# Gating the prompt rows of an expert's output on VectorE as they leave the accumulators, instead of in the combine, with six norm buffers instead of three

## The chip, the cores and the metric

The kernel runs on one core of one Trainium2 chip. The metric is the device time of one execution in microseconds; smaller is better.

## The reference, cut to what matters

One layer of a decoder trunk for two groups of requests: 1024 prompt rows and 64 sample rows (8 requests of 8 tokens), each of width 1024. Its second half is a mixture of 16 experts with two experts a row, followed by a post-norm:

```
h2 = x * (1 + sc2) + sh2
ff = moe(h2)                 # two experts a row, weights w
x  = layer_norm(ALPHA * x + (1 + g2) * ff, ln_g[1], ln_b[1])
expert: (silu(x @ w_gate[e]) * (x @ w_up[e])) @ w_down[e]
```

The gate `1 + g2` is a vector of 1024 numbers. All prompt rows share one; the sample rows have one for each of the eight requests. It is linear, so that it can be applied to each expert's output row or to the weighted sum of the two.

## The kernel before, in words

The program is a row of blocks, each with one hand-written instruction order for each engine. The last two are touched.

**block_experts (from line 2472).** The rows that chose an expert are packed into *slots* of 128 rows; there are 23 slots here. Every slot has one expert, an expert has one slot or more. All products are made in pieces of float32 split into a high and a low part (the high part is a cast, the low part the difference), three passes for each step of 128. TensorE's loop over the slots (2599 to 2608) is: the gate product of slot s (bank 0), the transposes of the hidden rows a of slot s-1, the up product of slot s (bank 1), the transposes of x for slot s+1, and the down product of slot s-1 (banks 2 and 3). So the down product of a slot runs in the next round of the loop.

ScalarE's `slot` (2645) does silu of the gate product, the high part of aT, the high part of x, and `y_part` (2635), which copies banks 2 and 3 into the staging rows `y` and issues their store to `y_d` in HBM. VectorE's `slot` (2702) does the low part of aT, the product `a` = up x silu, and the low part of x.

In the last slot of each expert both engines also split the next expert's weights (`among(0)`, `among(1)`, `among(2)` for gate, up and down): ScalarE casts two halves of 128x2048 (2622), and VectorE, once each cast half is there, subtracts (2681). The first expert's weights are split ahead of the loop in `first`. SP loads expert e+1's raw weights (2461) when VectorE is through with a part of expert e. After the last expert SP loads the second norm's scale and offset and the gate vector (2537), and the residual rows (2540), into the space of the raw weights. TensorE waits for the low part of x before a gate product, and for the low part of aT and for both copies of `y` (`y_act`, `y_second`) before a down product.

**block_combine (from line 2718).** There are nine tiles of 128 rows, eight of the prompt and one of the sample rows (64). POOL gathers the two expert outputs of each row by 18 indirect DMAs (2766) and then issues the eight outputs (2773): DMAs that add to an output which already holds the norm's offset. Tiles 0 and 1 are weighted and summed by VectorE (2817, 2818), tiles 2 to 8 by TensorE with diagonal matrices that ScalarE prepares (2757, 2781). Then, tile by tile, VectorE multiplies by the gate (2824), adds ALPHA times the residual and takes the row sum (2828); ScalarE makes mean and variance (2793 to 2799); VectorE, one tile behind, subtracts the mean and multiplies by the norm's scale into one of three norm buffers (2838) and takes a reciprocal (2844); ScalarE scales (2787) and POOL writes out. From tile 3 on, line 2838 waits until the output three tiles earlier has landed. The sample tile's offset is added by VectorE (2847), and SP writes it (2866). TensorE waits for the gate multiply four tiles back (2754) before it reuses a pair of banks.

Of the kernel before, what the change touches and what calls it, by code (L numbers as in the profile page):

```python
# [28 lines left out]
P = 128  # L29
D = 1024  # L30
# [165 lines left out]
def memory_experts(c):  # L196

    c.w_lo2, c.x_parts, c.a_parts = allocate(
        c, 1, ("w_lo2", 2 * PART, F32R), ("x_parts", 2 * D, F32R), ("a_parts", 2 * DE, F32R))


def memory_combine(c):

    c.combine, = allocate(c, 2, ("combine", 2 * NT * D + 7 * D + 64 + NT * 2 * P, F32))


def setup(nc, ctx, t):
# [69 lines left out]
    c.modw_in = [c.sem(f"modw_in{s}") for s in range(5)]  # L277
# [7 lines left out]
    o = 0  # L285
# [2186 lines left out]
def block_experts(c):  # L2472
# [16 lines left out]
    c.v_in = sem("v9_in")  # L2489
    hi_done = c.hi_done  # L2490
# [36 lines left out]
    with nc.Block() as block:  # L2527
        @block.sync
        def _(sp):
            with sp.Fori(1, NE) as e:  # L2530
                load_expert(c, sp, e)
# [82 lines left out]
        def _(act):  # L2614
# [20 lines left out]
            def y_part(s):  # L2635

                act.wait_ge(down_done, s + 1)
                act.wait_ge(y_out, s * 16 + 16)
                act.copy(y[:, 0:512], c.bank(2)).then_inc(y_act, 1)
                act.copy(y[:, 512:], c.bank(3)).then_inc(y_second, 1)  # L2640
                act.wait_ge(y_act, s + 1)
                act.wait_ge(y_second, s + 1)
                act.dma_start(c.y_d[bass.ds(s * MB, MB), :], y).then_inc(y_out, 16)

            def slot(s, among):
# [3 lines left out]
                aT_part(s)  # L2649
                among(0)  # L2650
# [8 lines left out]
            def first():  # L2659
                x_part(0)  # L2660
                for h in range(2):
# [6 lines left out]
            aT_part(n)  # L2668
            y_part(n)
# [4 lines left out]
        def _(dve):  # L2674
# [20 lines left out]

            def first():
                split(0, 0, 0, None, (1,))
                x_part(0)
                split(1, 0, 0, None)
                split(2, 0, 0, None)  # L2700

            def slot(s, among):
# [6 lines left out]
                among(1)  # L2709
                among(2)  # L2710
# [4 lines left out]
            aT_part(slots(dve))  # L2715


def block_combine(c):
# [4 lines left out]
    def part(n, count=1):  # L2723
# [4 lines left out]
    nrm = [part(2 * RY + 2 + s) for s in range(3)]  # L2728
    g2s = part(2 * RY + 5)
    x1 = c.raw[:, 0:NT * D].rearrange("p (i d) -> p i d", i=NT)  # L2730
    lng2, lnb2, g2 = (c.raw[:, D * (NT + n):D * (NT + n + 1)] for n in range(3))
    o = (2 * RY + 6) * D
    squares = part(2 * RY + 6)
# [4 lines left out]
    n_ready, scaled, sample_out = sem("n9_ready"), sem("n9_scaled"), sem("y9_sample")  # L2738
    y_in = [sem(f"y9_in{s}") for s in range(RY)]
    done = [sem(f"y9_out{s}") for s in range(3)]  # L2740
    b_done, d_done, y_sum, g2_done, sum_ready, less_done, squared, var_ready, eps_set, link = (
        sem(n) for n in ("b9_done", "d9_done", "y9_sum", "g29_done", "m9_ready", "less9_done", "s9_squared", "v9_ready", "e9_set", "l9"))
# [3 lines left out]
    with nc.Block() as block:  # L2746
        @block.tensor
        def _(pe):
            for i in range(ON_DVE, NT):
# [3 lines left out]
                if i >= 4 + ON_DVE:  # L2753
                    pe.wait_ge(g2_done, i - 3)
# [7 lines left out]
        def _(pool):  # L2762
# [8 lines left out]
            for i in range(smp):  # L2771
                pool.wait_ge(scaled, i + 1)
                pool.dma_start(t["o_y_p"][0, i * P:(i + 1) * P, :], nrm[i % 3], accum_op=ALU.add).then_inc(done[i % 3], 16)

        @block.scalar
        def _(act):
            act.wait_ge(shares, 1)
            for i in range(ON_DVE, NT):
# [3 lines left out]
                a.then_inc(d_done, 1)  # L2782
            act.wait_ge(eps_set, 1)

            def scale(i):
                act.wait_ge(n_ready, i + 1)
                act.activation(nrm[i % 3], nrm[i % 3], ACT.Identity, scale=st[:, 24 * (i % 2) + 16:24 * (i % 2) + 17]).then_inc(scaled, 1)
# [16 lines left out]
        def _(dve):  # L2804
# [7 lines left out]
            def residual(i):  # L2812
                T = tile_rows(i)
                ac = acc[i % 2][0:T, :]
                if i < ON_DVE:
                    dve.wait_ge(y_in[i], 32)
                    linked(dve.tensor_scalar(ac, yy[i][0][0:T, :], c.xw[0:T, i, 0:1], None, ALU.mult))
                    linked(dve.scalar_tensor_tensor(out=ac, in0=yy[i][1][0:T, :], scalar=c.xw[0:T, i, 1:2], in1=ac,
# [5 lines left out]
                dve.tensor_tensor(ac, total, (g2 if i < smp else g2s)[0:T, :], ALU.mult).then_inc(g2_done, 1)  # L2824
                dve.wait_ge(g2_done, i + 1)
# [88 lines left out]
```

## Time and profile before

| | us |
|---|---|
| median of 3 runs | 1234.09 (1234.07 to 1236.64) |
| the profiled execution's own time | 1233.19 |
| its span, first to last instruction | 1231.4 |
| TensorE (PE) busy | 1106.6 (90%) |
| VectorE (DVE) busy | 731.9 (59%) |
| ScalarE (ACT) busy | 587.6 (48%) |
| GpSimd (POOL) busy | 127.0 (10%) |
| mean granted TensorE clock | 0.961 of 2.4 GHz |

Busy time is summed over the whole span. The expert loop runs from about 748 to 1170 us, the combine from about 1173 us to the end.

### The profile page before, as it was taken

What the parts mean: (1) busy time and instruction counts of PE and PEld (TensorE: products, weight loads), DVE (VectorE), ACT (ScalarE), POOL (GpSimd) and SP (SyncE); (2) the same over time, 40 slices, a digit from 0 to 9 for tenths busy, and PEclk for the clock granted to TensorE, in tenths of its full rate; (3) what the DMA queues carried; (4) which work ended last, traced back from release to release, by engine and by line L of the source; (5) the groups of instructions that cost most, each with busy time, mean ns of one, the idle gap of its engine ahead of it and who ended that gap; (6) DMA issues with size and microseconds to landing.
All of it is one profiled execution on the core that took longest, in us unless ns stands there. A gap on an engine that the chain in (4) does not pass through costs nothing. (4 is left out here: it accounts for less than half of the span.)

```text
span 1231.4 us, 20687 instructions
## 1 busy us (share of the span) xinstructions
PE 1106.6 (90%) x7413; PEld 898.3 (73%) x7414; DVE 731.9 (59%) x1433; ACT 587.6 (48%) x1022; POOL 127.0 (10%) x203
## 2 busy tenths in 40 slices
PE   5899999998799999999799927999999999999843
PEld 3898779987566777777587716888888888888621
DVE  1641351342656677776677679885575497556166
ACT  0641101214467767666432245865465576645154
POOL 0321420010100000000000011100000010000061
PEclk9999999999899999999999957999999999999977
DMA  9574773072598000000433368996696699683488
GB/s 348 201 205 156 268 258 125 1 106 71 160 338 196 2 2 2 1 2 1 140 137 120 121 247 313 399 397 245 224 392 220 215 401 399 238 341 123 158 311 150
DMA packets 93111, 238.07 MB, mean 193 GB/s; under 512 B 9430, under 2 KB 18837, under 8 KB 93007
## 3 DMA queue, kind: packets, MB, share of 16 engines
q1 hardware_dynamic: 76921, 189.93, 44.6%
q0 software_dynamic: 10288, 31.20, 8.2%
q10 hardware_dynamic: 5830, 15.99, 3.7%
q8 instruction: 45, 0.74, 0.3%
q14 instruction: 27, 0.22, 0.1%
HBM read 199.04 MB, written 44.33 MB: 198 GB/s over the span
## 5 line engine op out<-in xcount | busy, mean ns | idle before, releaser
L2569 PE MATMUL psum<-w_hi,x_parts 128*128 128x512 f32 x736 | 239.5, 397 | 5.6 <-DVE x_parts L2688 5.6
L2681 DVE TENSOR_TENSOR w_lo<-raw,w_hi 128x2048 fp32r<-128x2048 f32 x95 | 213.3, 2287 | 38.9 <-ACT w_hi L2622 38.0
L2622 ACT CAST w_hi<-raw 128x2048 fp32r<-128x2048 f32 x90 | 168.0, 1920 | 9.5 <-ACT work L2640 9.2
L2569 PEld LDWEIGHTS psum<-w_hi,x_parts 128*128 128x128 f32 x736 | 139.7, 190 | 35.3 <-issue 6.2
L2569 PE MATMUL psum<-w_lo,x_parts 128*128 128x512 f32 x368 | 144.6, 393 | 0.0
L2569 PE MATMUL psum<-w_hi,a_parts 128*128 x368 | 120.3, 398 | 4.0 <-DVE a_parts L2694 4.0
L1763 DVE CUSTOM_DVE_ANT_0 low<-psum,high 128x512 f32<-128x512 f32 (+5 forms) x172 | 92.2, 579 | 37.3 <-PE psum L1451 23.5
L1649 ACT ACTIVATE low<-low,high 128x640 f32<-128x640 f32 (+9 forms) x140 | 98.9, 710 | 10.9 <-DVE high L1763 10.8
L1481 PE MATMUL psum<-keep,low 128*128 128x128 f32 (+1 forms) x556 | 92.3, 286 | 12.1 <-ACT high L1710 6.1
L1676 ACT COPY high<-psum 128x512 f32<-128x512 f32 (+3 forms) x128 | 63.7, 502 | 76.5 <-PE psum L1481 76.3
L716 PE MATMUL psum<-h_hi,l_parts 128*128 128x384 f32 (+1 forms) x384 | 94.1, 328 | 0.0
L2042 PE MATMUL psum<-wo_parts,mix_parts 128*128 128x512 f32 x384 | 93.1, 399 | 0.0
L1481 PEld LDWEIGHTS psum<-keep,low 128*128 128x128 f32 (+1 forms) x556 | 59.8, 140 | 42.5 <-issue 27.4
L2042 PEld LDWEIGHTS psum<-wo_parts,mix_parts 128*128 128x128 f32 x384 | 72.1, 191 | 17.0 <-issue 2.1
L2569 PEld LDWEIGHTS psum<-w_hi,a_parts 128*128 128x128 f32 x368 | 70.0, 190 | 18.2 <-issue 4.2
L2569 PEld LDWEIGHTS psum<-w_lo,x_parts 128*128 128x128 f32 x368 | 69.9, 190 | 14.1
L1499 PE MATMUL psum<-high 128*64 128x128 f32 x1056 | 72.3, 280 | 1.2 <-ACT low L1695 0.7
L2569 PE MATMUL psum<-w_lo,a_parts 128*128 x184 | 72.4, 394 | 0.0
L716 PEld LDWEIGHTS psum<-h_hi,l_parts 128*128 128x128 f32 x384 | 67.6, 188 | 0.7 <-issue 0.4
L2627 ACT CAST x_parts<-psum 128x512 fp32r<-128x512 f32 x48 | 25.8, 590 | 86.5 <-PE psum L2561 86.5
L676 PE MATMUL psum<-l_parts,h_hi 128*128 128x384 f32 (+3 forms) x288 | 64.6, 315 | 1.1 <-DVE h_lo L946 1.1
L1499 PEld LDWEIGHTS psum<-high 128*64 128x64 f32 x1056 | 56.6, 137 | 11.4 <-issue 8.8
(384 smaller groups left out, 1753.5 us busy)
## 6 DMA issues: line engine op xcount, KB each, us to landing
raw<-in_moe_w_gate SPq DMA_DIRECT2D x32, 1024.0 KB, 9.2
raw<-in_moe_w_up SPq DMA_DIRECT2D x32, 1024.0 KB, 9.9
raw<-in_moe_w_down SPq DMA_DIRECT2D x32, 1024.0 KB, 9.1
top<-in_w_mod SPq DMA_DIRECT2D x8, 2048.0 KB, 8.4
y_d<-work ACTq DMA_DIRECT2D x24, 512.0 KB, 6.2
low<-in_w_mod SPq DMA_DIRECT2D x4, 2048.0 KB, 18.9
high<-in_x_prompt SPq DMA_DIRECT2D x16, 512.0 KB, 3.7
y_d<-high SPq DMA_DIRECT2D x1, 8192.0 KB, 24.3
```

What stands on the lines that cost most here:

```text
L676: mm = pe.matmul(stage_bank(n)[0:T, 0:WIDTHS[st]], h_parts[left][:, k, at:at + T], right[:, k, :], start=(k == 0 and left == 0 and right i ...
L716: mm = pe.matmul(piece_bank(pc)[:, 0:w], left[:, k, :], h_parts[right][:, k, toks], start=(k == 0 and left is hi and right == 0), stop=(k ...
L1481: mm = pe.transpose(turn_bank(what)[0:w, (k - 4 * m) * P:(k - 4 * m + 1) * P], pb[n % 3][:, g, k * P:k * P + w], c.ident)
L1499: mm = pe.matmul(c.bank(6 + br)[HD * g:HD * g + HD, j * P:(j + 1) * P], c.vs[:, k0 + k, br, g, :], pT[n % 2][:, g, k, :], start=(k == 0), ...
L1649: act.activation(x, x, ACT.Exp, bias=mx[:, at + g:at + g + 1], scale=-1.0, accum_out=sums[g]).then_inc(e_ev, 1)
L1676: act.copy(dst[:, 0:w], src[:, 0:w]).then_inc(r_act, 1)
L1763: dve.tensor_tensor_reduce(pb[n % 3][:, g, at * P:at * P + cols], c.bank(2 * g + q % 2)[:, 0:cols], bias, -1.0, least if m else 3e38, ALU. ...
L2042: mm = pe.matmul(c.bank(2 * (s % 2) + n), mixed[i % 2][l][:, k, :], wo[w][:, k, n * 512:(n + 1) * 512], start=(k == 0 and l + w == 0), sto ...
L2569: mm = pe.matmul(out, left[l][:, k * P:(k + 1) * P], w[:, bass.ds(at - o + k * step, 512)], start=n == 0, stop=n == len(steps) - 1)
L2622: act.copy(c.w_hi[:, at:at + PART // 2], c.raw[:, o:o + PART // 2]).then_inc(hi_done[p], 1)
L2627: ins = act.copy(xT[0][:, 512 * h:512 * h + 512], c.bank(4 + h))
L2681: dve.tensor_tensor(low, c.raw[:, o:o + PART // 2], c.w_hi[:, at:at + PART // 2].bitcast(F32), ALU.subtract).then_inc(c.lo_done[p], 1)
```

## The change

The gate of the prompt rows moves from the combine into the expert stage. A slot holds prompt rows and sample rows, so a table `row_kind` holds, for each slot and row, a 1 or a 0 for "prompt" and the opposite for "sample". ScalarE writes the multiplier rows (gate for a prompt row, 1 for a sample row) into the staging rows `y`, once the previous store of `y` has landed; VectorE multiplies banks 2 and 3 by them in place. ScalarE only waits and issues the store. The gate vector has a buffer of its own and is loaded at the head of SP's queue of the block. In the combine the gate multiply stays for the sample tile alone, the residual reads the accumulators directly, one multiply of tile 1 goes to ScalarE, and there are six norm buffers. Some semaphores are declared in another way, since more of them are needed.

```diff
+    c.gate_row, c.row_kind = allocate(c, 0, ("gate_row", D, F32), ("row_kind", 2 * (MAX_SLOTS + 1), F32))
...
         @block.sync
         def _(sp):
+            sp.dma_start(c.gate_row, row_broadcast(c.mod_d, 5 * D, D)).then_inc(g2_in, 16)
             with sp.Fori(1, NE) as e:
                 load_expert(c, sp, e)
...
-            for n, src in enumerate((row_broadcast(t["ln_g"], D, D), row_broadcast(t["ln_b"], D, D),
-                                     row_broadcast(c.mod_d, 5 * D, D))):
+            for n, src in enumerate((row_broadcast(t["ln_g"], D, D), row_broadcast(t["ln_b"], D, D))):
...
 (ScalarE)
             def y_part(s):
-                act.wait_ge(down_done, s + 1)
-                act.wait_ge(y_out, s * 16 + 16)
-                act.copy(y[:, 0:512], c.bank(2)).then_inc(y_act, 1)
-                act.copy(y[:, 512:], c.bank(3)).then_inc(y_second, 1)
                 act.wait_ge(y_act, s + 1)
                 act.wait_ge(y_second, s + 1)
                 act.dma_start(c.y_d[bass.ds(s * MB, MB), :], y).then_inc(y_out, 16)
+            def gate_rows(s):
+                act.wait_ge(y_out, s * 16 + 16)
+                act.activation(y, c.gate_row, ACT.Identity, scale=is_prompt[:, bass.ds(s, 1)],
+                               bias=is_sample[:, bass.ds(s, 1)]).then_inc(gated, 1)
             def slot(s, among):
...
                 aT_part(s)
+                gate_rows(s)
                 among(0)
...
             def first():
                 x_part(0)
+                act.wait_ge(g2_in, 16)
+                act.wait_ge(kinds_set, 1)
...
             aT_part(n)
+            gate_rows(n)
             y_part(n)
 (VectorE)
+            def y_part(s):
+                dve.wait_ge(down_done, s + 1)
+                dve.wait_ge(gated, s + 1)
+                dve.tensor_tensor(y[:, 0:512], c.bank(2), y[:, 0:512], ALU.mult).then_inc(y_act, 1)
+                dve.tensor_tensor(y[:, 512:], c.bank(3), y[:, 512:], ALU.mult).then_inc(y_second, 1)
             def first():
                 split(0, 0, 0, None, (1,))
                 x_part(0)
+                dve.memset(is_prompt[:, 0:1], 1.0)
+                dve.memset(is_sample[:, 0:1], 0.0)
+                dve.tensor_scalar(is_prompt[:, 1:], c.ids_i[:, 0:MAX_SLOTS], float(SEQ), None, ALU.is_lt)
+                dve.tensor_scalar(is_sample[:, 1:], c.ids_i[:, 0:MAX_SLOTS], float(SEQ), None, ALU.is_ge).then_inc(kinds_set, 1)
...
                 x_part(s + 1)
                 among(1)
+                y_part(s)
                 among(2)
...
             aT_part(slots(dve))
+            y_part(slots(dve))
 (combine)
-    nrm = [part(2 * RY + 2 + s) for s in range(3)]
+    NN = 6
+    nrm = [part(2 * RY + 2 + s) for s in range(NN)]
+    reused = NT - NN
...
                 if i >= 4 + ON_DVE:
-                    pe.wait_ge(g2_done, i - 3)
+                    pe.wait_ge(sum_ready, i - 3)
...
+            act.wait_ge(y_in[1], 32)
+            act.activation(yy[1][0], yy[1][0], ACT.Identity, scale=c.xw[:, 1, 0:1]).then_inc(half_sum, 1)
...
-                    linked(dve.tensor_scalar(ac, yy[i][0][0:T, :], c.xw[0:T, i, 0:1], None, ALU.mult))
+                    if i == 0:
+                        linked(dve.tensor_scalar(first, first, c.xw[0:T, i, 0:1], None, ALU.mult))
+                    else:
+                        dve.wait_ge(half_sum, 1)
...
-                dve.tensor_tensor(ac, total, (g2 if i < smp else g2s)[0:T, :], ALU.mult).then_inc(g2_done, 1)
-                dve.wait_ge(g2_done, i + 1)
+                if i == smp:
+                    linked(dve.tensor_tensor(ac, total, g2s[0:T, :], ALU.mult))
+                    total = ac
                 dve.wait_ge(c.x1_in[i], 32)
...
-                dve.scalar_tensor_tensor(out=ac, in0=x1[0:T, i, :], scalar=ALPHA, in1=ac, op0=ALU.mult, op1=ALU.add,
+                dve.scalar_tensor_tensor(out=ac, in0=x1[0:T, i, :], scalar=ALPHA, in1=total, op0=ALU.mult, op1=ALU.add,
                                          accum_out=q[:, 0:1]).then_inc(sum_ready, 1)
...
-                if i >= 3:
-                    dve.wait_ge(done[i % 3], 16 * (i // 3))
+                if i >= NN:
+                    dve.wait_ge(done[i - NN], 16)
```

## Rows read from the trace of the kernel before

**Rows 1.** The page: the span, and the costliest group of ScalarE in the expert loop.
```profile
span 1231.4 us, 20687 instructions
PE 1106.6 (90%) x7413; PEld 898.3 (73%) x7414; DVE 731.9 (59%) x1433; ACT 587.6 (48%) x1022; POOL 127.0 (10%) x203
...
L2622 ACT CAST w_hi<-raw 128x2048 fp32r<-128x2048 f32 x90 | 168.0, 1920 | 9.5 <-ACT work L2640 9.2
```

**Rows 2.** Window (us, busy of PE, PEld, DVE, ACT, POOL, PEclk, DMA, GB/s), then TensorE's timeline.
```profile
984.00:1002.00 18.00, 18.00 (x87) 14.97 (x86) 16.06 (x11) 14.42 (x13) 1.83 (x2) 1.00 1.03 397
...
997.03 0.39 PE L2569 MATMUL psum<-w_hi,x_parts 128*128 128x512 f32 x1
...
1009.21 0.48 PE L2569 MATMUL psum<-w_hi,a_parts 128*128 x1
...
1014.75 0.39 PE L2569 MATMUL psum<-w_hi,x_parts 128*128 128x512 f32 x1
```

**Rows 3.** ScalarE's timeline (start, duration, what, [idle before <-releaser]): plain, then split slot.
```profile
867.78 1.07 ACT L2627 CAST x_parts<-psum 128x512 fp32r<-128x512 f32 x2 [5.74 <-PE psum L2561]
...
997.32 0.59 ACT L2639 COPY work<-psum 128x512 f32<-128x512 f32 x1 [0.84 <-PE psum L2569]
...
998.62 0.35 ACTq L2643 DMA_DIRECT2D y_d<-work  x1
999.01 3.72 ACT L2622 CAST w_hi<-raw 128x2048 fp32r<-128x2048 f32 x2 [0.62 <-ACT work L2640]
1002.68 0.60 ACT L2648 ACTIVATE work<-psum 128x512 f32<-128x512 f32 x1
...
1003.64 3.74 ACT L2622 CAST w_hi<-raw 128x2048 fp32r<-128x2048 f32 x2
```

**Rows 4.** VectorE's timeline in the same split slot.
```profile
1000.95 4.50 DVE L2681 TENSOR_TENSOR w_lo<-raw,w_hi 128x2048 fp32r<-128x2048 f32 x2 [1.76 <-ACT w_hi L2622]
1005.36 0.68 DVE L2694 TENSOR_TENSOR a_parts<-psum,a_parts 128x512 fp32r<-128x512 f32 x1
1005.97 4.48 DVE L2681 TENSOR_TENSOR w_lo<-raw,w_hi 128x2048 fp32r<-128x2048 f32 x2
...
1010.97 1.28 DVE L2688 TENSOR_TENSOR x_parts<-psum,x_parts 128x512 fp32r<-128x512 f32 x2
1012.41 4.49 DVE L2681 TENSOR_TENSOR w_lo<-raw,w_hi 128x2048 fp32r<-128x2048 f32 x2 [0.16 <-ACT w_hi L2622]
```

**Rows 5.** Timeline of the combine: TensorE's products, VectorE's wait, and its last tiles.
```profile
1186.03 26.02 PE L2757 MATMUL psum<-combine 128*128 128x512 f32 x56 [17.68 <-DMA combine<-y_d,dest_y]
...
1206.23 1.29 DVE L2838 SCALAR_TENSOR_TENSOR combine<-combine,raw 128x1024 f32<-128x1024 f32 x1 [4.81 <-DMA out_o_y_p<-combine]
...
1216.44 1.23 DVE L2828 SCALAR_TENSOR_TENSOR combine<-raw,combine 128x1024 f32<-128x1024 f32 x1
...
1218.99 1.20 DVE L2824 TENSOR_TENSOR combine<-psum,combine 64x1024 f32<-64x1024 f32 x1
```

**Rows 6.** Windows of the combine's output traffic (last two columns: DMA share, GB/s).
```profile
1199.00:1200.00 1.00, 1.00 (x4) 0.44 (x3) 1.00 (x2) 0.97 (x4) 0.08 (x1) 1.00 1.07 176
...
1204.00:1205.00 1.00, 1.00 (x4) 0.50 (x3) 0.00 (x0) 0.00 (x0) 0.00 (x0) 1.00 1.02 201
...
1215.00:1220.00 5.00, 0.00 (x0) 0.00 (x0) 4.90 (x8) 3.99 (x10) 0.86 (x1) 0.50 0.92 134
```

**Rows 7.** Timeline of the combine: ScalarE's scaling of a normalised tile.
```profile
1191.75 1.13 ACT L2787 ACTIVATE combine<-combine 128x1024 f32<-128x1024 f32 x1
```

**Rows 8.** Timeline at the start of the expert loop, then a window.
```profile
758.61 4.49 DVE L2681 TENSOR_TENSOR w_lo<-raw,w_hi 128x2048 fp32r<-128x2048 f32 x2 [1.04 <-ACT w_hi L2622]
...
765.04 0.49 PE L2569 MATMUL psum<-w_hi,x_parts 128*128 128x512 f32 x1 [3.07 <-DVE x_parts L2688]
...
765.00:770.00 5.00, 4.96 (x15) 3.94 (x16) 4.41 (x2) 4.33 (x4) 0.00 (x0) 0.66 1.04 387
```

**Rows 9.** All 24 stores of the staging rows, from issue to landing.
```profile
DMA to landing us min/median/max: 2.6/6.2/8.3
```

More of the change, by code:

```diff
@@ L275, in setup @@
     c.modT = c.misc[:, 0:144].rearrange("p (a b) -> p a b", a=2 * KT)
-    c.modw_in = [c.sem(f"modw_in{s}") for s in range(5)]
+    c.modw_in = [early_sem(f"modw_in{s}") for s in range(5)]
     c.modb_in, c.mod_half_done = c.sem("modb_in"), c.sem("mod_half_done")
@@ L2489, in block_experts @@
     c.v_in = sem("v9_in")
+    g2_in, kinds_set, gated = sem("g2_in"), sem("kinds_set"), sem("y_gated")
+    is_prompt, is_sample = (c.row_kind[:, (MAX_SLOTS + 1) * n:(MAX_SLOTS + 1) * (n + 1)] for n in range(2))
     hi_done = c.hi_done
@@ L2727, in block_combine @@
     acc = [part(2 * RY + s) for s in range(2)]
-    nrm = [part(2 * RY + 2 + s) for s in range(3)]
-    g2s = part(2 * RY + 5)
+    NN = 6
+    nrm = [part(2 * RY + 2 + s) for s in range(NN)]
+    g2s = part(2 * RY + 2 + NN)
     x1 = c.raw[:, 0:NT * D].rearrange("p (i d) -> p i d", i=NT)
-    lng2, lnb2, g2 = (c.raw[:, D * (NT + n):D * (NT + n + 1)] for n in range(3))
-    o = (2 * RY + 6) * D
-    squares = part(2 * RY + 6)
+    lng2, lnb2 = (c.raw[:, D * (NT + n):D * (NT + n + 1)] for n in range(2))
+    o = (2 * RY + 3 + NN) * D
+    squares = part(2 * RY + 3 + NN)
     o += D
@@ L2737, in block_combine @@
     diag = c.combine[:, o + 64:o + 64 + NT * 2 * P].rearrange("p (i k q) -> p i k q", i=NT, k=2)
-    n_ready, scaled, sample_out = sem("n9_ready"), sem("n9_scaled"), sem("y9_sample")
+    n_ready, scaled, sample_out, once_out = sem("n9_ready"), sem("n9_scaled"), sem("y9_sample"), sem("y9_once")
     y_in = [sem(f"y9_in{s}") for s in range(RY)]
-    done = [sem(f"y9_out{s}") for s in range(3)]
-    b_done, d_done, y_sum, g2_done, sum_ready, less_done, squared, var_ready, eps_set, link = (
-        sem(n) for n in ("b9_done", "d9_done", "y9_sum", "g29_done", "m9_ready", "less9_done", "s9_squared", "v9_ready", "e9_set", "l9"))
+    reused = NT - NN
+    done = [sem(f"y9_out{s}") for s in range(reused)]
+    b_done, d_done, y_sum, sum_ready, less_done, squared, var_ready, eps_set, link, half_sum = (
+        sem(n) for n in ("b9_done", "d9_done", "y9_sum", "m9_ready", "less9_done", "s9_squared", "v9_ready", "e9_set", "l9", "h9_sum"))
     smp = NP_TILES
@@ L2772, in _ @@
                 pool.wait_ge(scaled, i + 1)
-                pool.dma_start(t["o_y_p"][0, i * P:(i + 1) * P, :], nrm[i % 3], accum_op=ALU.add).then_inc(done[i % 3], 16)
+                pool.dma_start(t["o_y_p"][0, i * P:(i + 1) * P, :], nrm[i % NN],
+                               accum_op=ALU.add).then_inc(done[i] if i < reused else once_out, 16)
         @block.scalar
@@ L2786, in scale @@
                 act.wait_ge(n_ready, i + 1)
-                act.activation(nrm[i % 3], nrm[i % 3], ACT.Identity, scale=st[:, 24 * (i % 2) + 16:24 * (i % 2) + 17]).then_inc(scaled, 1)
+                act.activation(nrm[i % NN], nrm[i % NN], ACT.Identity, scale=st[:, 24 * (i % 2) + 16:24 * (i % 2) + 17]).then_inc(scaled, 1)
             for i in range(NT):
@@ L2865, in _ @@
             sp.wait_ge(b_done, 1)
-            sp.dma_start(t["o_y_s"].rearrange("b j d -> (b j) d"), nrm[smp % 3][0:NS, :]).then_inc(sample_out, 16)
+            sp.dma_start(t["o_y_s"].rearrange("b j d -> (b j) d"), nrm[smp % NN][0:NS, :]).then_inc(sample_out, 16)
             sp.wait_ge(c.out_done, c.out_total)
-            for s in range(3):
-                sp.wait_ge(done[s], 16 * ((smp - s + 2) // 3))
+            for s in range(reused):
+                sp.wait_ge(done[s], 16)
+            sp.wait_ge(once_out, 16 * (smp - reused))
             sp.wait_ge(sample_out, 16)
```

10 lines of the change are left out of this document (6 added, 4 removed).

## The prediction

> **What bounds the kernel now.** I read the page first: the span is 1231.4 us and TensorE is busy for nine tenths of it [rows 1]. The profiled execution took 1233.19 us, so 1.8 us lie around the span; the median of the three runs is 1234.09, 0.9 above it. About 0.2% (2.5 us) is what a measurement of this kernel can tell from no change.
>
> The change touches two stages, so I then asked for windows of each. In the expert loop TensorE is busy in all 18 us of the window shown, and a slot lasts 17.7 us, from one gate product (997.03) to the next (1014.75) [rows 2]. But VectorE is busy 16.1 of those 18 us too. It and ScalarE have spare time only in the mean. The reader should look there at the order of work, since both execute strictly in order. In a slot that also splits the next expert's weights (call it a *split slot*), ScalarE does silu, aT high, first weights (two halves), x high, second weights, two copies of the down result, the store's issue, third weights; VectorE does aT low, first, a, x low, second, third [rows 3, 4]. 90 ScalarE splits in the loop are 15 such slots [rows 1]; the other 8 of the 23 are *plain*, seen in the ScalarE timeline by 5.74 us of idle before the x cast in place of 2.1 [rows 3]. In order they are SSSS P S P SS P S P SSSS P SS P S P P: eight times a split slot follows directly on a split slot.
>
> The combine is the other way round: its ends are on VectorE. There TensorE's products run as one group of 26.02 us from 1186.03 and are over at 1212.05, yet VectorE takes the last tile at 1218.99 [rows 5], because each tile costs it a gate multiply, a residual and a normalisation, and it once waits 4.81 us for a norm buffer whose output write had not landed.
>
> **Combine, part by part.** *Removed:* the gate multiply of eight prompt tiles (1.21 us each), one of two operand multiplies of tile 1 (0.75, now ScalarE's, about 1.1, while VectorE works on tile 0), and with six norm buffers the 4.81 us wait, since tile 3 needs no buffer back. VectorE's round falls from 3.8 to 1.22 + 1.28 + 0.16 = 2.7 us [rows 5]. What is late next is TensorE: 26.02 us over seven tiles, less about 2 us at its slow start, are 3.43 us a tile. TensorE itself starts on the landing of tile 2's gathers, which nothing here moves: the gathers keep their place ahead of all outputs on POOL's queue. Its new wait (sum instead of gate multiply four tiles back) asks for tile 4 before tile 8: done near 1200, asked at 1208.6. So the last tile starts at 1212.15 instead of 1218.99. Behind it the order is unchanged (the sample tile keeps its multiply), so the end comes **6.8 us** earlier. Buffers again: tile 6 wants output 0 back at 1210, and it landed by 1206.2; outputs 1 and 2, queued right behind it, need 2.6 us each at the queued rate [rows 6], so they land by about 1211, and are wanted at 1214 and later.
>
> **Expert stage, part by part.** ScalarE loses two copies (1.2 us with their gap, from 997.32 on) and gains a 1024-wide scaled activation, as the combine's norm scaling: 1.13 us [rows 7], right behind aT high. VectorE gains two products from the accumulators, as its x low pair: 1.28 us [rows 4], behind the *second* weights. In sum little: the danger is the order. ScalarE's store, and everything behind it, now waits for VectorE's products, and these wait for VectorE's second weights (1012.41 to 1016.90), where ScalarE's copies (the like of 997.32, a slot later: 1015) ran as soon as the accumulators were ready. The third weights, silu, aT and the next first weights are queued behind that store on ScalarE, and VectorE waits in turn for their halves. That closes a ring. From the end X of x low: second weights X+4.6; gated products X+5.9; store issued and third weights begun on ScalarE X+6.6 (0.62 behind the copy now); two halves 3.67, silu and aT high 0.96, X+11.2; gate rows, X+12.3; first half of the next first weights 1.94, X+14.2; VectorE's two halves and a 5.00, x low 1.28: **X+20.4** [rows 3, 4]. TensorE's own slot is 17.71, so each of the eight direct successions costs 2.7 us: about 1.4 before the gate product (x low late) and 1.3 before the down product, which starts 12.2 us into the slot [rows 2], while aT low is ready at X+13.6.
>
> Before a run, a first split slot behind a plain one has its x low ready 1.5 us early (ring entered at silu, not at the store); after it, the next slot still loses the 1.3. So single split slots cost nothing, and a run of k about 2.7(k-1) - 0.2. Runs of 4, 2, 4, 2: 7.9 + 2.5 + 7.9 + 2.5 = 20.8.
>
> *Start.* TensorE waited 3.07 us for x low at 765.04, the end of a VectorE chain that had waited for ScalarE's first weights [rows 8]; the gate activation stands ahead of these: +1.0. The four small operations before the loop (0.06 to 0.2 us each) fit into the idle time there. The gate vector moves from late on SP's queue to its head, before expert 1's loads, 0.42 us of issue. It delays these by that, unseen since they are used some 12 us after their issue; ScalarE now waits for its landing. The stores of the same 512 KB land in 2.6 to 8.3 us [rows 9]; up to about 4 it is hidden behind x high, at 8.3 it would cost under 3 more. I take none. *Tail.* Two products on VectorE for two copies on ScalarE: 0.3. Lower bound for the stage: 20.8 + 1.0 + 0.3 = **22**, or 21 if the small gaps in the ring close.
>
> *The unknown: the store's landing.* The gate activation overwrites the staging rows, so it waits for the previous store, 5.1 us after its issue in the ring. The 24 stores landed in 2.6 to 8.3 us, median 6.2 [rows 9]; split slots have 6.2 to 8.3. At 2.7 nothing is added, at 6.2 1.1 us in each of eight rings (+9, in all 31), at 8.3 about +25. The loads that share the DMA engines with it (397 GB/s in the window) [rows 2] would be spread over a longer slot and stand some 2 us further ahead of the store, so I take a landing of about 5.5: +3, in all **25**.
>
> The Trainium skill, DMA: Bandwidth & Descriptors, Queues, rings and completion order, says that a DMA engine takes turns packet by packet between the queues that have work. By that rule the store, on ScalarE's queue beside SP's loads, would have half the rate and land in about 4 us (an estimate), the gate rows would never wait, and the sum would be 22. The landings [rows 9] are longer than that wherever loads run, so the rule is not what I count on.
>
> **Sum.** 25 - 6.8 = +18.2 on 1233.19 gives 1251.4; with the 0.9 us of the median, **1252.3**.
>
> **Rivals.**
> *Hidden anyway (faster).* ScalarE waits 2.1 and VectorE 1.8 us in every split slot now [rows 3, 4]; if their added 1.3 us went into those waits, TensorE would never notice, and the combine's gain would stand: 1234.1 + 1.3 - 6.8 = 1228.6. It decides at whether the gated products can run when the accumulators are ready. Against it: at that time VectorE is in the middle of its second weights. Chance 0.08.
> *The clock.* After 3.07 us of waiting the granted clock fell to its lower level (1.2 of 2.4 GHz) for part of the next 5 us, mean 0.66: up to 1.7 us lost [rows 8]. The new waits are 1.2 to 1.5 us, twice a slot. Inside a run the ring hides a slower TensorE; at the end of each of four runs it would cost 1.1 to 1.7: +5, 1257. For it speaks only that longer waits do it; waits this long in a busy stretch aren't in these rows. Chance 0.12. The Trainium skill, TensorE: Matmul & The Clock Gate, HAM oscillation, says that idle gaps between groups of products let the clock fall; by that this case is the one that comes.
> *Slow stores.* At 8.3 us the ring is 23.6 us: about 47 for the stage, 1274. Chance 0.08.
> *Output writes bind the combine.* Alone, each output keeps the DMA engines 0.92 busy over 3.8 us, 3.5 us of engine time; eight of them from about 1199, where the gathers' end lets the rate fall to 176 GB/s, would end near 1227, some 1.6 before those of now: 1257.5. Against it: when queued they moved 201 GB/s, 2.6 us for 0.52 MB, under TensorE's 3.43 [rows 6]. Chance 0.06.
> *No change within 0.2%.* It would need the ring to cost just 6.8, half a run: 0.03.
> The forecast itself, stage +21 to +31: 0.63.
>
> **Range.** The forecast's own is 1248 to 1258, which takes in the clock and the output rival. To hold the time 8 times in 10 it reaches up towards slow stores, 1268, and down to 1243, where the ring would cost half. Slower 0.89, the same 0.03, faster 0.08.
>
> **What would show it.** In the profile after: VectorE's two products right behind its second weights and not behind TensorE; ScalarE's third weights released by VectorE; TensorE waiting on x_parts and a_parts from VectorE some 8 to 12 times each, 1 to 2 us, where it waited twice and once; slots in a run 20.4 us or more apart, plain ones 17.7; a wait of the gate activation on the store or none. In the combine: no wait of the normalisation on an output, VectorE released by TensorE at each tile, 6.8 us from the last product's end less. I am wrong if TensorE does not wait in the runs, or if the last tile in the combine isn't taken right behind its product.

## The result, and the profile after

The changed kernel takes 1268.77 us (median of 4 runs, 1268.07 to 1274.83); the kernel before, run beside it, 1234.08 (4 runs, 1232.16 to 1236.64). The ratio is 1.0284, 95% interval 1.0255 to 1.0313. The forecast was 1252.3, that is +18.2 us, and +34.7 came, 0.8 us beyond the upper end of the range. The sign and the mechanism (a ring through ScalarE's queue) were right, and the size forecast was about half of what came.

The page of the profiled execution (1268.77 us), for [rows 1]. The group of line 2626 is ScalarE's weight splits.

```profile
span 1266.9 us, 20759 instructions
PE 1124.4 (89%) x7413; PEld 908.2 (72%) x7414; DVE 750.9 (59%) x1476; ACT 589.3 (47%) x999; POOL 132.4 (10%) x203
...
L2626 ACT CAST w_hi<-raw 128x2048 fp32r<-128x2048 f32 x90 | 167.2, 1910 | 85.2 <-DVE work L2710 85.2
```

The splits cost the same as before (167.2 us for 168.0), but ScalarE stood idle ahead of them for 85.2 us in place of 9.5, waiting for VectorE's gated product. VectorE's busy time grew by only 19 us, the span by 35.5: what has to be read is the order of work, not the total.

Where the time went: from the first gate product of the loop to the issue of the last store it is 421.45 us before (748.31 to 1169.76) and 463.4 after (746.92 to 1210.34), **+42.0**. From there to the end of the span it is 61.6 before and 56.5 after, **-5.1**. The rest, 1.4, is an earlier start of the loop in this profile; over all the profiles of this case that start lies anywhere from 746.9 to 751.7, so it is not put down to the change.

The chain of waits in the expert stage (engine, what it worked on, who released it: us in total, times, longest):

```profile
ACT w_hi L2626 <- DVE work L2710: 85.2, 15, 6.2
...
DVE w_lo L2691 <- ACT w_hi L2626: 76.1, 29, 3.5
...
ACT work L2648 <- DMA y_d<-work: 37.0, 16, 3.2
...
PE psum L2573 <- DVE x_parts L2698: 29.1, 10, 4.2
...
PE psum L2573 <- DVE a_parts L2704: 6.5, 3, 4.5
```

ScalarE waits for VectorE and VectorE for ScalarE: the ring. The third line is a link that the forecast had weighed and made too small: the gate activation waits for the previous store. TensorE waits ten times for x low instead of twice, and three times for aT low instead of once.

ScalarE in a run of split slots, for [rows 3] (start, duration, what, [idle before <-releaser]):

```profile
793.74 0.35 ACTq L2643 DMA_DIRECT2D y_d<-work  x1
794.13 3.72 ACT L2626 CAST w_hi<-raw 128x2048 fp32r<-128x2048 f32 x2 [6.18 <-DVE work L2710]
797.75 0.60 ACT L2654 ACTIVATE work<-psum 128x512 f32<-128x512 f32 x1
798.24 0.59 ACT L2637 CAST a_parts<-psum 128x512 fp32r<-128x512 f32 x1
801.61 1.24 ACT L2648 ACTIVATE work<-gate_row,row_kind 128x1024 f32<-128x1024 f32 x1 [2.79 <-DMA y_d<-work]
802.76 3.71 ACT L2626 CAST w_hi<-raw 128x2048 fp32r<-128x2048 f32 x2
...
816.80 0.35 ACTq L2643 DMA_DIRECT2D y_d<-work  x1
...
824.34 1.25 ACT L2648 ACTIVATE work<-gate_row,row_kind 128x1024 f32<-128x1024 f32 x1 [2.46 <-DMA y_d<-work]
...
839.53 0.34 ACTq L2643 DMA_DIRECT2D y_d<-work  x1
```

And VectorE in the same stretch, for [rows 4]:

```profile
810.89 4.48 DVE L2691 TENSOR_TENSOR w_lo<-raw,w_hi 128x2048 fp32r<-128x2048 f32 x2
815.30 0.68 DVE L2709 TENSOR_TENSOR work<-psum,work 128x512 f32<-128x512 f32 x1
815.90 0.68 DVE L2710 TENSOR_TENSOR work<-psum,work 128x512 f32<-128x512 f32 x1
819.14 4.49 DVE L2691 TENSOR_TENSOR w_lo<-raw,w_hi 128x2048 fp32r<-128x2048 f32 x2 [2.56 <-ACT w_hi L2626]
```

From store to store it is 23.1 and 22.7 us. The ring is the one forecast at 20.4, and the wait for the store stands in it besides: 2.79 and 2.46 us. In all eight direct successions the distance is the store's landing (6.65 to 7.70 us from its issue, mean 7.25) and 15.36 us more, to within 0.01. The eight last 22.0 to 23.1 us, 22.6 in the mean, instead of 17.7: 39 of the stage's 42 us. The rest is at its ends: the second gate product comes 1.8 us later after the first, and the last store 1.4 us later after the last gate product. A split slot that stands alone costs nothing: around it two slots last 35.43 us from silu to silu (858.83 to 894.26), 17.7 each.

TensorE, the timeline at three gate products of the first run and one of the second, and then windows (us, busy of the engines, granted clock, DMA share, GB/s):

```profile
788.05 0.49 PE L2573 MATMUL psum<-w_hi,x_parts 128*128 128x512 f32 x1 [3.03 <-DVE x_parts L2698]
...
811.12 0.79 PE L2573 MATMUL psum<-w_hi,x_parts 128*128 128x512 f32 x1 [3.47 <-DVE x_parts L2698]
...
833.84 0.79 PE L2573 MATMUL psum<-w_hi,x_parts 128*128 128x512 f32 x1 [2.17 <-DVE x_parts L2698]
...
927.31 0.49 PE L2573 MATMUL psum<-w_hi,x_parts 128*128 128x512 f32 x1 [3.11 <-DVE x_parts L2698]
...
940.83 0.49 PE L2573 MATMUL psum<-w_hi,a_parts 128*128 x1 [0.98 <-DVE a_parts L2704]
```
```profile
788.00:793.00 5.00, 4.95 (x15) 3.94 (x16) 5.00 (x4) 0.00 (x0) 0.00 (x0) 0.66 0.96 309
812.00:818.00 6.00, 6.00 (x18) 4.68 (x18) 4.58 (x4) 0.81 (x1) 0.00 (x0) 0.62 1.06 328
...
927.00:932.00 5.00, 4.69 (x21) 3.89 (x22) 5.00 (x4) 0.22 (x1) 0.00 (x0) 1.00 0.95 306
```

In the first run all of the wait comes at the gate product. With each of these waits the granted clock is at its lower level for some microseconds (1.2 of 2.4 GHz; means of 0.66 and 0.62), so that the up product ends later and the down product finds aT low ready: the second wait that was forecast, 1.3 us before each down product, is used up by slow products. Two gate products show the other case: at 927.31, after 3.11 us of waiting, and at 1065.28, after 1.70, the clock stays at 1.00, and there a wait of 0.98 us does stand before the next down product. So the length of a wait alone does not decide whether the clock falls; what else does was not tried.

The combine, VectorE's timeline and then TensorE's group, for [rows 5]:

```profile
1233.81 1.22 DVE L2860 SCALAR_TENSOR_TENSOR combine<-raw,psum 128x1024 f32<-128x1024 f32 x1 [4.04 <-PE psum L2781]
1234.96 0.08 DVE L2860 DVE_READ_ACCUMULATOR combine<-raw,psum 128x1 f32 x1
1234.96 1.28 DVE L2870 SCALAR_TENSOR_TENSOR combine<-combine,raw 128x1024 f32<-128x1024 f32 x1
...
1240.68 1.22 DVE L2860 SCALAR_TENSOR_TENSOR combine<-raw,psum 128x1024 f32<-128x1024 f32 x1 [0.81 <-PE psum L2781]
```
```profile
1227.23 27.28 PE L2781 MATMUL psum<-combine 128*128 128x512 f32 x56 [18.44 <-DMA combine<-y_d,dest_y]
```

As forecast, VectorE follows TensorE tile by tile, 3.43 us apart, and waits for no norm buffer. From the end of TensorE's group to the end of the span it is 12.4 us in place of 19.3, 7.0 less. But the group is 27.28 us long in place of 26.02, and it ends 44.2 us after the last store's issue (1254.5), where it was 42.3 (1212.05).

### The profile page after: what moved, and what is told of

Same layout as the page of the kernel before. It is cut to its first block and busy times, and to the rows that moved or that the text cites. A ratio compares the mean times of both kernels' runs of the same rounds, so it can differ in the third digit from the quotient of the medians.

```text
span 1266.9 us, 20759 instructions
## 1 busy us (share of the span) xinstructions
PE 1124.4 (89%) x7413; PEld 908.2 (72%) x7414; DVE 750.9 (59%) x1476; ACT 589.3 (47%) x999; POOL 132.4 (10%) x203
## 5 line engine op out<-in xcount | busy, mean ns | idle before, releaser
L2573 PE MATMUL psum<-w_hi,x_parts 128*128 128x512 f32 x736 | 249.7, 412 | 29.1 <-DVE x_parts L2698 29.1
L2626 ACT CAST w_hi<-raw 128x2048 fp32r<-128x2048 f32 x90 | 167.2, 1910 | 85.2 <-DVE work L2710 85.2
L2573 PEld LDWEIGHTS psum<-w_hi,x_parts 128*128 128x128 f32 x736 | 145.5, 198 | 64.4 <-issue 33.1
L2573 PE MATMUL psum<-w_lo,x_parts 128*128 128x512 f32 x368 | 149.2, 406 | 0.0
L2573 PEld LDWEIGHTS psum<-w_hi,a_parts 128*128 128x128 f32 x368 | 70.3, 191 | 21.3 <-issue 7.2
L2573 PEld LDWEIGHTS psum<-w_lo,x_parts 128*128 128x128 f32 x368 | 73.3, 199 | 14.9
L1453 PE MATMUL psum<-score_parts 64*128 64x512 f32 (+3 forms) x528 | 63.7, 365 | 0.0
```

The lines of the kernel that those rows point to most:

```text
L1453: mm = pe.matmul(c.bank(2 * g + q % 2)[:, 0:w * P], left[rows, j, :], right[rows, br, keys], start=n == 0, stop=n == 2)
L2573: mm = pe.matmul(out, left[l][:, k * P:(k + 1) * P], w[:, bass.ds(at - o + k * step, 512)], start=n == 0, stop=n == len(steps) - 1)
L2626: act.copy(c.w_hi[:, at:at + PART // 2], c.raw[:, o:o + PART // 2]).then_inc(hi_done[p], 1)
```

## The experiments

Theory: the ring on ScalarE's in-order queue costs the stage its 42 us, with the gate activation's wait for the store inside it, and the combine's part is a gain. Rivals: the lower clock is the main cost; the combine's part gains nothing; the new work on VectorE and ScalarE costs by itself. The runs were made in three groups, each beside the kernel before, and each ratio is to the kernel before of its own group: 1234.64 us for the first four runs, 1233.14 for the next three and 1234.91 for the last. "Stage" below is from the first gate product to the last store's issue, "end" from there to the end of the span: 421.45 and 61.6 before, 463.4 and 56.5 after.

**Six buffers alone.** The kernel before, with

```diff
-    nrm = [part(2 * RY + 2 + s) for s in range(3)]
+    NN = 6
+    nrm = [part(2 * RY + 2 + s) for s in range(NN)]
```

> The kernel before with six norm buffers in the combine and nothing else; the gate multiplies stay there. Theory (VectorE's order bounds the combine before): the 4.8 us wait of the normalisation of tile 3 goes, VectorE's round stays 3.8 us, so the time falls by 4.8 us to about 1229.3. Rival (output writes bound the end of the combine): the outputs queue up, the wait moves to the end, and the time falls by 1.6 us or less, to 1232.5 or more.

Measured: 1230.57 us, ratio 0.9959 (0.9930 to 0.9987). Stage 422.0, end 58.5. That is 4.1 us less, nearer to the theory's 4.8 than to the rival's 1.6. The wait on an output is gone, and the end is 3.1 us shorter; TensorE's group is 27.44 us here, 1.4 longer than in the profile before, and from its end on 5.1 us are saved, the wait of 4.81 and a little more. This part of the change is a small gain on its own.

**Three buffers in the changed kernel.**

```diff
-    NN = 6
+    NN = 3
```

> The changed kernel with three norm buffers instead of six, the gate still in the expert stage. Theory: the normalisation of tile 3 waits again for output 0, some 5 us, but VectorE's round of 2.7 us under TensorE's 3.43 us a tile catches up 0.7 us a tile over five tiles, so the end is 1 to 3 us later than in the changed kernel: about 1271. Rival (VectorE is the bound as before): the whole wait of 4.8 us is lost, 1273.6 or more.

Measured: 1271.98 us, ratio 1.0324 (1.0273 to 1.0374). The normalisation waits for outputs again, 3.62, 0.96 and 1.20 us, yet the end is 57.4, 0.9 later than with six, and the stage (463.6) the same: the theory's case, at the low end. With the gate multiplies gone VectorE catches up, so the buffers shorten the end by 3.1 us without that part of the change and by 0.9 with it: their gains don't add.

**No wait for the store.** ScalarE does the gate activation into an unused accumulator bank, and VectorE multiplies by the gate vector itself.

```diff
-                act.wait_ge(y_out, s * 16 + 16)
-                act.activation(y, c.gate_row, ...)
+                for h, done in enumerate((half_gated, gated)):
+                    act.activation(c.bank(7), c.gate_row[:, 512 * h:512 * h + 512], ...)
+                    act.wait_ge(done, s + 1)
...
 (VectorE)
+                dve.wait_ge(y_out, s * 16 + 16)
-                dve.tensor_tensor(y[:, 0:512], c.bank(2), y[:, 0:512], ALU.mult)
+                dve.tensor_tensor(y[:, 0:512], c.bank(2), c.gate_row[:, 0:512], ALU.mult)
```

> The changed kernel with the wait on the store out of ScalarE's chain: its gate activations (two of 512 columns, the same work) go to an accumulator bank that nothing reads, and VectorE multiplies by the plain gate vector, so that the sample rows' outputs are gated as prompt rows; the order of the rest is the same. Theory (a ring of 20.4 us in successive split slots, lengthened by the wait for the store to 22.7 to 23.1): slots in a run fall back to about 20.4 us, the stage costs 21 to 24 us more than before instead of 42, total about 1250. Rival (the ring is slow for another reason, such as loads that arrive late or the lower clock): slots in a run stay near 22.7 us and the total near 1268.

Measured: 1257.27 us, ratio 1.0204 (1.0156 to 1.0251). From store to store it is 20.73 to 20.79 us in the eight successions, where 20.4 was worked out; the two half-wide activations take 1.60 us from start to end instead of 1.24, and 1.72 instead of 1.15 up to the start of the next cast, which is more than the rest. The stage is 450.2, end 56.2. TensorE's waits in its profile:

```profile
PE psum L2574 <- DVE x_parts L2700: 17.7, 9, 4.8
PE psum L2574 <- DVE a_parts L2706: 12.0, 9, 4.2
```

In the runs of split slots they are 1.46 to 1.50 us before the gate product and 0.96 to 0.99 before the down product, and the clock stays up: this is the picture that the prediction drew (1.4 and 1.3). So the ring without the store's wait is within 0.4 us of what it was said to be, and taking that wait out is worth 13 us of stage: 1.9 less in each of eight successions, 15 in all, of which some 2 are given back. The stage is still 28.8 us longer than before, not 21 to 24, and the time is 7 us above what was expected of this run. Part of that belongs to the detour: the start waits 4.79 us in place of 4.19, and a split slot behind a plain one, which costs nothing in the changed kernel, takes 0.4 here (silu to silu over two slots 35.80 us for 35.43), six times.

**The gate activation later**, behind x high instead of ahead of the first weights.

```diff
                 aT_part(s)
-                gate_rows(s)
                 among(0)
                 act.wait_ge(up_done, s + 1)
                 x_part(s + 1)
+                gate_rows(s)
```

> The changed kernel with ScalarE's gate activation moved behind its high part of x, out of the way of the first weights; all the rest as it is. Theory: the activation (1.15 us) and the wait for the store leave the ring, which is then 19.3 us, 1.6 over TensorE's slot: the stage costs about 18 us more than before, total about 1245. Rival (only the move of the products to VectorE costs, the place of the activation does not matter): total near 1268. Second rival (the ring is nothing, store traffic is all): total near 1229.

Measured: 1245.90 us, ratio 1.0100 (1.0057 to 1.0143), as expected. From store to store 19.44 to 19.50 us, stage 439.85, end 56.0. The activation now comes 9.5 us behind the store's issue, where it could have started 5.1 behind it, and in the loop it waits for nothing. TensorE's waits are 0.98 us before the down product and 0.20 before the gate product, and the clock is 1.00 behind them:

```profile
798.98 0.50 PE L2573 MATMUL psum<-w_hi,a_parts 128*128 x1 [0.99 <-DVE a_parts L2704]
...
804.91 0.49 PE L2573 MATMUL psum<-w_hi,x_parts 128*128 128x512 f32 x1 [0.20 <-DVE x_parts L2698]
```

What is left of the ring, 1.7 us in each succession, is the store ahead of the third weights.

**The store later too**, behind the third weights. These wait for the down product themselves, so that the store doesn't stand in for that.

```diff
                 among(1)
-                y_part(s)
+                act.wait_ge(down_done, s + 1)
                 among(2)
+                y_part(s)
```

> The changed kernel with both steps taken out of ScalarE's way: the gate activation behind the high part of x, and the store's issue (with its wait for VectorE's products) behind the third weights, which wait for the down product alone. Theory (the ring runs over the third weights queued behind the store, and over the gate activation ahead of the first weights): no ring is left, slots in a run are 17.7 us, the stage costs within 1 us of before, and the combine's gain of 5 to 7 us is seen: about 1228. Rival (VectorE has no room for 1.3 us more in a split slot, whatever the order): slots in a run stay above 18.5 us and the total is 1235 or more.

Measured: **1230.43 us** (12 runs), ratio 0.9975 (0.9958 to 0.9991) of the kernel before: 2.7 us faster, and 38 under the change as it was made. Expected was 1228. Stage 422.97, 1.5 us longer than before, end 55.9. ScalarE in a run:

```profile
795.50 0.60 ACT L2654 ACTIVATE work<-psum 128x512 f32<-128x512 f32 x1 [3.01 <-issue]
...
796.46 3.73 ACT L2626 CAST w_hi<-raw 128x2048 fp32r<-128x2048 f32 x2
800.75 1.08 ACT L2631 CAST x_parts<-psum 128x512 fp32r<-128x512 f32 x2 [0.57 <-PE psum L2565]
801.71 1.26 ACT L2648 ACTIVATE work<-gate_row,row_kind 128x1024 f32<-128x1024 f32 x1
802.86 7.35 ACT L2626 CAST w_hi<-raw 128x2048 fp32r<-128x2048 f32 x4
810.72 0.35 ACTq L2643 DMA_DIRECT2D y_d<-work  x1
```

Second and third weights run back to back (x4), no weight split waits for VectorE, and TensorE's gate products come every 17.7 us, in plain and split slots alike. TensorE waits twice for x low and once for aT low, as before. All of the new arithmetic is in this kernel, so it costs 1.5 us of stage at the most; the other 40 of the change were its place. Six buffers alone (the first run, 1230.57) are as fast: with the gate moved in this way too, the end is 2.5 us shorter but the stage 1 us longer, and the two times can't be told apart.

**The store later, the gate activation as in the change.** The diff of the last run, without that of the one before it.

> The changed kernel with only the store's issue behind the third weights; the gate activation stays ahead of the first weights. Theory: the store now starts later, just before silu, and the gate activation that follows waits for its whole landing of 7 to 8 us, so the ring is hardly shorter than in the changed kernel: total 1255 to 1268. Rival (only ScalarE's queue behind the products costs): the total falls to about 1230.

Measured: 1274.76 us, ratio 1.0318 (1.0288 to 1.0348). That is above the 1255 to 1268 expected, and no better than the change itself: its four runs lie from 1268.03 to 1274.83, those of the change from 1268.07 to 1274.83. Stage 466.7, end 56.4. The expectation said that the store would start later. It doesn't: it is issued 0.2 us behind VectorE's products, as in the changed kernel (819.40 behind their end at 819.18; there 816.80 behind 816.58). What moved is the third weights, which used to fill the time until the store had landed; now the gate activation waits 3.57, 4.50 and 4.71 us in the first three successions instead of 2.30, 2.79 and 2.46. The distances are 22.0 to 23.8 us, 22.7 in the mean, and each is again the store's landing (6.6 to 8.4 us) and 15.35 more. So once the gate activation waits for the store, the third weights are off the ring, and moving them ahead of the store buys nothing; it pays only with the gate activation moved as well.

**Products first.** With the gate activation behind x high, VectorE does the gated products ahead of the second weights.

```diff
 (VectorE)
                 x_part(s + 1)
+                y_part(s)
                 among(1)
-                y_part(s)
```

> The changed kernel with the gate activation behind the high part of x, and VectorE's gated products ahead of its second weights instead of behind them; ScalarE's store stays where it is. Theory: ScalarE's third weights start as early as in the kernel before, the ring is gone; VectorE's second weights end some 3 us later, right when the up product asks for them, which costs 0 to 0.5 us a split slot: total 1228 to 1234. Rival (VectorE's waiting for the accumulators ahead of its second weights delays everything): 1245 or more, no better than with the gate activation moved alone.

Measured: 1234.42 us, ratio 1.0013 (0.9993 to 1.0033). From store to store 17.85 to 17.86 us in seven of the eight successions (19.88 in the first, behind the start of the loop), stage 425.5, end 56.6. The time is at the upper end of what was expected and can't be told from the kernel before. The ring opens from VectorE's side as well: the store goes when the accumulators are ready, as ScalarE's copies let it before. A rest of 0.15 us in each split slot stays.

**Half of the store.** What is behind the landing of 7 to 8 us: the store's own bytes or a fixed wait?

```diff
-                act.dma_start(c.y_d[bass.ds(s * MB, MB), :], y)
+                act.dma_start(c.y_d[bass.ds(s * MB, MB), 0:512], y[:, 0:512])
...
                 among(2)
+                act.dma_start(c.y_d[bass.ds(s * MB, MB), 512:], c.gate_row[:, 512:])
```

> The changed kernel, but the store that the gate activation waits for holds only the first 512 of 1024 columns; the other half of the bytes goes out by a DMA of its own behind the third weights, from the constant gate vector, so that the second half of each expert's output rows isn't the reference's. Same bytes in all, same place of the gate activation. In the changed kernel the stores of a run of split slots landed 7.2 to 8.1 us after their issue, and the gate activation waited 1.9 to 3.2 us. Theory (the landing grows with the store's own bytes, which share the DMA engines with the weights being loaded): the half lands in about 4 us, ahead of the high part of aT, the gate activation waits for nothing, the run's store-to-store distance falls from 22.7 to 23.1 us to about 20.4 and the time to about 1248 (2.5 us by 8 successions less). Rival (the landing is mostly a fixed wait behind transfers queued before it, whatever its size): the half still lands in 6 us or more, the gate activation still waits over 1 us, distance 22 to 23, time 1259 to 1269.

Measured: 1265.88 us, ratio 1.0234 (1.0206 to 1.0262). Over all the slots in which loads were running, the half store landed in 5.9 to 7.4 us, 6.6 in the mean, where the whole store of the changed kernel took 6.7 to 8.1, 7.3 in the mean: 0.7 us less. The activation waited 1.0 to 2.5 us behind each split slot, and the eight distances are 21.3 to 22.6, 22.0 in the mean, each its landing and 15.35 more. Time, wait and landing are the rival's. But the run did not separate the two as it was meant to. The other half stands behind the third weights in the program, yet ScalarE issued it 0.56 us behind the first, while the casts were still running:

```profile
796.12 0.34 ACTq L2644 DMA_DIRECT2D y_d<-work  x1
796.51 1.91 ACT L2627 CAST w_hi<-raw 128x2048 fp32r<-128x2048 f32 x1 [6.17 <-DVE work L2717]
796.68 0.34 ACTq L2647 DMA_DIRECT2D y_d<-gate_row  x1
```

So the same bytes were in one queue at about the same time as before, and in smaller packets: 144 packets carried the whole store of the changed kernel, and 288 the two halves (the changed kernel from 798.0 to 801.1, the half store from 799 to 805; queue, packets, MB, share of the 16 engines in that time; q10 carries the stores, q1 SP's weight loads):

```profile
q10 hardware_dynamic: 144, 0.52, 41.3%
...
q10 hardware_dynamic: 288, 0.52, 22.7%
```

A half is then as many packets as the whole was, and a landing that goes by the number of packets would have fallen as little as one that is a fixed wait. The same view, one microsecond at a time, shows what the landing is made of. The changed kernel, whose store was issued at 793.74, in the microseconds from 796 and from 799:

```profile
q1 hardware_dynamic: 86, 0.17, 99.2%
...
q10 hardware_dynamic: 69, 0.27, 64.8%
q1 hardware_dynamic: 74, 0.15, 38.4%
```

The half store, issued at 796.12, in the microseconds from 799 and from 801:

```profile
q1 hardware_dynamic: 156, 0.32, 91.7%
...
q1 hardware_dynamic: 110, 0.22, 56.8%
q10 hardware_dynamic: 94, 0.18, 46.5%
```

In the changed kernel the store's first packet comes 4.3 us behind its issue, in the half store 3.9. The queue then takes its turns with the loads, packet for packet (69 beside 74, 94 beside 110 in the microseconds shown), and the 512 KB are through in 2.6 to 3.5 us. That is a dead time ahead of the first packet while loads run: 3.5 to 4.4 us in both kernels, while the loads' queue moves 1.0 to 1.4 MB, and it is over half of the landing. The kernel before has it too, with 3.2 to 3.7. What sets it wasn't tried. A plain slot's store (890.32), with no load pair in flight, had its first packet after 0.85 us and landed in 2.6 us in all.

## Why the prediction was right, and where it was wrong

**The mechanism: right.** ScalarE's third weights released by VectorE's products, VectorE waiting for ScalarE's halves, plain and single split slots at 17.7 us, eight direct successions that carry the cost: all are in the trace. Taking out the store's wait left a ring of 20.7 us against 20.4 worked out from single rows, and with gate activation and store in another place the same work ran at the old pace of 17.7. In the prediction's terms the ring is 5.1 us from the store's issue to the gate activation and 15.3 from there to the next store; where the activation waits, the 5.1 becomes the landing. Measured, the second part is 15.36.

**The failed step: the store's landing**, "I take a landing of about 5.5: +3". Measured in the eight rings: 6.65 to 7.70 us, 7.25 in the mean, so 1.8 to 2.8 us of wait in each and 18.7 us over eight, where 3 were booked. The stage is +42.0, not +25; of these 17 us the landing is nearly 16, and the two ends of the stage are the rest. The reason given for 5.5 was that a longer slot puts the loads further ahead of the store. But SP's loads hang on VectorE's splits, which are part of the ring, and move with it: in the run of after SP issues the pair for the second weights from 813.34 to 815.91, and the store follows at 816.80; in before it issues them from 802.30 to 804.87, and the store falls in between, at 803.76:

```profile
813.34 2.57 SPq L2463 DMA_DIRECT2D raw<-in_moe_w_up  x2
...
802.30 2.57 SPq L2461 DMA_DIRECT2D raw<-in_moe_w_up  x2
...
803.76 0.35 ACTq L2643 DMA_DIRECT2D y_d<-work  x1
```

The 6.2 to 8.3 us that split slots had [rows 9] were there to be used as they stood. The very eight stores that stand in the rings took 6.21 to 8.33 us before, 6.96 in the mean; by the prediction's own arithmetic that is +15 in place of +3 and a total of 1264. The "slow stores" rival took 8.3 for all of them, with 47 for the stage and 1274, and got a chance of 0.08.

**The rule of the Trainium skill.** Taking turns packet by packet was to bring the store home in about 4 us. The rule itself (the Trainium skill, DMA: Bandwidth & Descriptors, Queues, rings and completion order) is borne out once the store moves, with 69 packets of its queue beside 74 of the loads' in one microsecond. As a price of a landing it fails, since 3.5 to 4.4 us go by before the first packet. Not counting on it was right.

**TensorE's waits: there, but in another form.** Forecast were x_parts and a_parts, 1 to 2 us, 8 to 12 times each. There were ten and three. Those for x_parts lasted 1.70 to 4.19 us from the second gate product on, and wherever the clock fell behind one, no wait for a_parts followed. With the ring at 20.7 the forecast's form came out: nine of each, among them seven of 1.5 us for x_parts and eight of 1.0 for a_parts.

**The clock rival.** In the changed kernel the clock falls with seven of the nine later waits at a gate product, but it is a follower: in the run the ring, not TensorE, sets the pace. The succession with the gate product at 927.31, where the clock stayed up, lasts 22.58 us, its landing of 7.22 and the same 15.36 as the others. Without the store's wait and with the gate later the waits in the successions were 1.5 us and less, the clock stayed up, and the ring's cost was still there. The Trainium skill, TensorE: Matmul & The Clock Gate, HAM oscillation, says that idle gaps between groups of products let the clock fall; the traces agree for most of the changed kernel's waits of 2.2 us and more (not for the one of 3.11), and not for those of 1.7 and less.

**The start: right.** +1.0 was forecast, and the wait at the second gate product is 4.19 us for 3.07 [rows 8]; with slower products ahead of it that gate product comes 1.8 us later. The gate vector's landing held ScalarE up for 1.6 us once, unseen, as taken. The tail was put at 0.3, and from the last gate product to the last store it is 32.4 us for 31.0, +1.4; the clock is at its lower level for 6.8 us there instead of 3.4.

**The combine: 6.8 forecast, 5.1 measured.** The steps hold (no wait on an output, the last tile taken right behind its product), and behind the last product the 6.8 came as 7.0. What failed is that TensorE's group was held at 26.02 us and at its place behind the last store: it took 27.28 and ended 1.9 us later, counted from that store. The other profiles, six buffers alone among them, have 26.99 to 27.44, so the 26.02 of the one profile before was the odd one. There the clock was low for the group's first 3.2 us, in the profile after for 5.8: its mean in the five microseconds from 1189 was 0.97, against 0.70 from 1230 in the profile after. That alone is worth 1.3 us, the whole difference in length.

**Hidden anyway, output writes, no change:** none came. The argument against the first, that VectorE is in the middle of its second weights when the accumulators are ready, held for the kernel before but not for the ring: there the down product was over at 807.65, and VectorE began its second weights at 810.89. With the products ahead of the second weights and the gate activation later the time came to 1234.42, and with gate activation and store later to 1230.43, near the 1228.6 of this rival: it describes another order of the same work.

## What to carry to other kernels

When work moves from one in-order engine to another, write down each engine's queue in the tightest slot and look for a closed walk: here store behind product behind split behind cast behind store. Its length, not busy time, is the slot, and one wait in it counts as often as slots follow on each other. A store's landing is then a term of the ring: take it as measured, from the rows of the very stores that will stand there, and put whatever reuses the buffer as late as its own use allows. The same arithmetic in another order was worth 38 us.

## What the hardware showed that was not expected

- A store of 512 KB issued on ScalarE's queue beside a stream of loads on SP's landed in 6.7 to 8.1 us. One of 256 KB, in as many packets of half the size and with another right behind it, took 5.9 to 7.4. In both, 3.5 to 4.4 us passed before the first packet. With no loads in flight the 512 KB took 2.6, with the first packet after 0.85.
- In the changed kernel's runs of slots TensorE's granted clock fell to its lower level with seven waits of 2.17 to 4.19 us in an otherwise dense stream (means of 0.62 and 0.66 in the windows shown), and stayed up with one of 3.11 and one of 1.70. In the half store run it fell with one of 1.83. With waits of 1.5 us and less in the expert loop it stayed up in every run.
- A DMA that stands behind two casts in ScalarE's program, with no semaphore between, was issued at 796.68, 0.17 us after the first of them began and 3.5 before the second ended.
- An activation of 1024 columns took 1.24 us from SBUF with row-wise scale and offset; the same in two halves into an accumulator bank, the second waiting for the first, took 1.60.
